# The RG-LRU mixer of a four-layer kernel: convolution through PSUM, Tanh for Sigmoid, low parts and the gelu product on GpSimd

## The reference

```python
def rglru_mixer(u, w_in, b_in, conv_w, conv_b, w_gx, b_gx, w_ga, b_ga, lam, w_out, b_out):
    proj = u @ w_in + b_in
    ybr = jax.nn.gelu(proj[..., :LRU_WIDTH])
    xbr = causal_dwconv(proj[..., LRU_WIDTH:], conv_w, conv_b)      # 4 taps
    xh = xbr.reshape(bsz, s, LRU_HEADS, LRU_BLOCK)                  # 10 heads of 128
    gx = sigmoid(einsum('bshi,hij->bshj', xh, w_gx).reshape(...) + b_gx)
    ga = sigmoid(einsum('bshi,hij->bshj', xh, w_ga).reshape(...) + b_ga)
    log_a = 8.0 * ga * log_sigmoid(lam)
    a_t = exp(log_a)
    b_t = sqrt(-expm1(2.0 * log_a)) * gx * xbr
    _, h = associative_scan(_linear_combine, (a_t, b_t), axis=1)    # h = a_t * h_prev + b_t
    return (h * ybr) @ w_out + b_out
```

## Time and profile before

| | us |
|---|---|
| median of three runs | 3145.37 |
| lowest and highest run | 3143.47, 3150.71 |
| the profiled execution, its own time | 3148.56 |
| its span | 3146.7 |
| TensorE busy | 2977.8 (95%) |
| VectorE busy | 1379.6 (44%) |
| ScalarE busy | 1194.0 (38%) |
| GpSimd busy | 1352.2 (43%) |

### The profile page before, as it was taken

One profiled execution on the slowest core, in us unless ns is written; L12 is line 12 of the kernel. 1 busy time (PEld: TensorE's weight loads), 2 busy tenths in 40 slices (PEclk: granted clock), 3 DMA queues, 4 the chain that ended last, 5 costly groups with the idle time before them and its releaser, 6 DMA issues.

```text
span 3146.7 us, 33766 instructions
## 1 busy us (share of the span) xinstructions
PE 2977.8 (95%) x13508; PEld 2440.9 (78%) x13508; DVE 1379.6 (44%) x2011; ACT 1194.0 (38%) x1658; POOL 1352.2 (43%) x724
## 2 busy tenths in 40 slices
PE   8899999999999788999999996999999989999998
PEld 6777777888887566888888785987888867778886
DVE  6655406523532683551352356653313345433132
ACT  5434436423433464542343432014323334343232
POOL 5333454444445366444444446005444432144443
PEclk9999999999999889999999997579999989999999
DMA  3211132232232222323332230002333321022322
GB/s 133 70 59 46 35 107 87 94 99 96 96 99 74 70 68 80 101 95 99 94 101 94 80 101 27 1 21 88 96 97 101 90 68 57 28 94 91 104 89 85
DMA packets 74172, 253.12 MB, mean 80 GB/s; under 512 B 8352, under 2 KB 8352, under 8 KB 74016
## 3 DMA queue, kind: packets, MB, share of 16 engines
q1 hardware_dynamic: 73008, 247.55, 24.4%
q10 hardware_dynamic: 1008, 3.41, 0.3%
HBM read 248.83 MB, written 2.10 MB: 80 GB/s over the span
## 4 chain that ended last, share of the span: by engine, by line
PE 86%; DVE 7%; ACT 3%; DMA 1%; issue 1%; POOL 1%; POOLq 0%; DVEq 0%; ACTq 0%; SPq 0%
PE bank L374 22%; PE bank L375 22%; PE bank L376 22%; PE bank L1660 3%; PE bank L396 2%; PE bank L397 2%; PE bank L398 2%; PE bank L855 1%; PE bank L857 1%; PE bank L856 1%; POOL wlo L2356 1%; PE bank L936 1%; DVE bank L1189 1%; DVE lth L1505 1%; ACT whi L319 1%
## 5 line engine op out<-in xcount | busy, mean ns | idle before, releaser
L2356 POOL TENSOR_TENSOR wlo<-raw,whi 128x1024 fp32r<-128x1024 f32 (+2 forms) x497 | 1133.5, 2283 | 1685.9 <-ACT whi L319 1685.8
L319 ACT ACTIVATE whi<-raw 128x1024 fp32r<-128x1024 f32 (+2 forms) x497 | 500.1, 1007 | 1126.5 <-DMA raw<-in_f_up 487.9
L374 PE MATMUL bank<-h_hi,whi 128*128 128x512 f32 x2240 | 880.2, 393 | 9.2 <-DVE h_lo L1956 3.4
L375 PE MATMUL bank<-h_lo,whi 128*128 128x512 f32 x2240 | 874.4, 390 | 0.0
L376 PE MATMUL bank<-h_hi,wlo 128*128 128x512 f32 x2240 | 873.4, 390 | 0.0
L374 PEld LDWEIGHTS bank<-h_hi,whi 128*128 128x128 f32 x2240 | 422.3, 189 | 102.1 <-DVE h_lo L1956 4.2
L375 PEld LDWEIGHTS bank<-h_lo,whi 128*128 128x128 f32 x2240 | 422.3, 189 | 89.2 <-issue 2.2
L376 PEld LDWEIGHTS bank<-h_hi,wlo 128*128 128x128 f32 x2240 | 422.3, 189 | 88.4
L374 PE MATMUL bank<-act_hi,whi 128*128 128x512 f32 x864 | 336.2, 389 | 0.9 <-POOL wlo L2356 0.9
L376 PE MATMUL bank<-act_hi,wlo 128*128 128x512 f32 x864 | 336.1, 389 | 0.0
L375 PE MATMUL bank<-act_lo,whi 128*128 128x512 f32 x864 | 336.1, 389 | 0.0
(11 more groups left out here) (451 smaller groups left out, 3802.9 us busy)
## 6 DMA issues: line engine op xcount, KB each, us to landing
raw<-in_f_up SPq DMA_DIRECT2D x216, 512.0 KB, 3.5
raw<-in_f_dn SPq DMA_DIRECT2D x64, 512.0 KB, 3.4
raw<-in_ssd_xbc SPq DMA_DIRECT2D x24, 512.0 KB, 3.5
raw<-in_f_dn SPq DMA_DIRECT2D x32, 384.0 KB, 3.0
raw<-in_lru_in SPq DMA_DIRECT2D x20, 512.0 KB, 3.5
raw<-in_ev_in SPq DMA_DIRECT2D x20, 512.0 KB, 3.5
raw<-in_f_dn SPq DMA_DIRECT2D x32, 320.0 KB, 2.9
raw<-in_ssd_z SPq DMA_DIRECT2D x16, 512.0 KB, 3.5
```

What stands on the lines that cost most here:

```text
L319: act.activation(whi[:, s, 0:WIDTH[u]], raw[:, s, 0:WIDTH[u]], ACT.Copy).then_inc(hi_done, 1)
L374: pe.matmul(out, wh, hi, start=kt == 0, stop=False)
L375: pe.matmul(out, wh, lo, start=False, stop=False)
L2356: pool.tensor_tensor(wlo[:, s, 0:n], raw[:, s, 0:n], whi[:, s, 0:n].bitcast(F32), ALU.subtract)\
```

## The change

- The convolution runs in the bank. ScalarE writes `ltap` with three zero columns ahead of it, waits for this, and writes the first tap with the bias back into the bank; VectorE adds three taps with the bank as one operand, and the last writes `xbr` and frees the bank.
- `low_x` moves from VectorE to GpSimd, and GpSimd's order in the stage's first part is written out around it.
- Sigmoid(x) becomes (1 + Tanh(x/2)) / 2, with the halves folded into the constants, `gated`, `decay` and `root`.
- `high_x` stands ahead of the weight split in ScalarE's order. Decays 0 to 3 move up among the x tiles, as do `one_minus` 0 and 1.
- The constants of lambda are computed in the SSD stage (VectorE: before tile 12 there) and kept in a place of their own. `lsq` moves to the place of another stage's tile.
- The product of scan and gelu moves to GpSimd, two blocks ahead of its low part. The scan is still written to SBUF.

The core of the diff (the lambda steps in the SSD stage, which are the old ones at new places, are cut):

```diff
-        ltap = at("ltap", BIG + 80 * KB, [P, 2, T])
-        lsq = at("lsq", BIG + 84 * KB, [P, 2, T])
+        ltap = at("ltap", BIG + 80 * KB, [P, 2, T + 4])
+        lsq = at("lsq", place["sqg"], [P, 2, T])
...
+        def lam_dve(dve, own):
...
+            own.link(dve.tensor_scalar(bias, bias, 0.5, None, ALU.mult))
+            own.link(dve.tensor_scalar(v0, v, 4.0, None, ALU.mult))
+            dve.tensor_scalar(u, v, -4.0, None, ALU.mult).then_inc(l_lam, 1)
...
+                elif t == 12:
+                    lam_dve(dve, own)
...
-            def sigmoids(g):
+            def tanhs(g):
...
-                        act.activation(b, b, ACT.Sigmoid, bias=col("lru_bgx", h)).then_inc(l_sg, 1)
+                        act.activation(b, b, ACT.Tanh, bias=col("lru_bgx", h), scale=0.5).then_inc(l_sg, 1)
                     else:
-                        act.activation(ga[:, h, :], b, ACT.Sigmoid, bias=col("lru_bga", h)).then_inc(st.free(t), 1)
+                        act.activation(ga[:, h, :], b, ACT.Tanh, bias=col("lru_bga", h), scale=0.5).then_inc(st.free(t), 1)
...
+            act.wait_ge(l_lam, 5)
             for j in range(NL):
                 st, t = l_in[j]
+                if j >= 2:
+                    high_x(j - 2)
                 if j in (5, 7, 9):
-                    sigmoids(j // 2 - 2)
+                    tanhs(j // 2 - 2)
                 act.wait_ge(l_u, j + 1)
                 w(act, l_x, j - 1)
-                act.activation(ltap[:, j % 2, :], st.bank(t)[:], ACT.Identity, bias=col("lru_bx", j)).then_inc(st.free(t), 1)
+                own.link(act.activation(ltap[:, j % 2, 3:T + 3], st.bank(t)[:], ACT.Identity, bias=col("lru_bx", j)))
+                act.activation(st.bank(t)[:], ltap[:, j % 2, 3:T + 3], ACT.Identity, bias=col("lru_conv", 5 * j + 4),
+                               scale=col("lru_conv", 5 * j + 3)).then_inc(l_tap, 1)
                 in_ahead(j)
-                if j >= 2:
-                    high_x(j - 2)
-            sigmoids(3)
+                if j in (6, 8):
+                    decay(j - 6)
+                    decay(j - 5)
             high_x(NL - 2)
+            tanhs(3)
             high_x(NL - 1)
-            act.wait_ge(l_lam, 4)
-            for k in range(3):
-                decay(k)
+            decay(4)
+            decay(5)
             in_ahead(10)
-            for k in range(3, 6):
-                decay(k)
-            in_ahead(11)
-            sigmoids(4)
             decay(6)
             decay(7)
-            in_ahead(12)
+            in_ahead(11)
+            tanhs(4)
             decay(8)
             decay(9)
+            in_ahead(12)
...
             def conv(j):
                 st, t = l_in[j]
-                st.freed(dve, t)
-                src, cv = ltap[:, j % 2, :], xbr[:, j, :]
-                own.link(dve.tensor_scalar(cv, src, col("lru_conv", 5 * j + 3), col("lru_conv", 5 * j + 4), ALU.mult,
-                                           ALU.add))
+                b = st.bank(t)[:]
+                dve.wait_ge(l_tap, j + 1)
                 for n in (1, 2, 3):
-                    ins = dve.scalar_tensor_tensor(out=xbr[:, j, n:T], in0=ltap[:, j % 2, 0:T - n],
-                                                   scalar=col("lru_conv", 5 * j + 3 - n), in1=xbr[:, j, n:T],
-                                                   op0=ALU.mult, op1=ALU.add)
+                    ins = dve.scalar_tensor_tensor(out=xbr[:, j, :] if n == 3 else b, in0=ltap[:, j % 2, 3 - n:T + 3 - n],
+                                                   scalar=col("lru_conv", 5 * j + 3 - n), in1=b, op0=ALU.mult, op1=ALU.add)
...
-                        ins.then_inc(l_x, 1)
...
+                        ins.then_inc(st.free(t), 1)
+                st.freed(dve, t)
+                dve.engine_nop().then_inc(l_x, 1)
...
-                own.link(dve.tensor_tensor_scan(out=lth[:, k, :], data0=ga[:, k, :], data1=xbr[:, k, :], initial=0.0,
-                                                op0=ALU.mult, op1=ALU.add))
-
-            def product(k):
-                dve.wait_ge(l_y, k + 1)
-                dve.tensor_tensor(lth[:, k, :], lth[:, k, :], ybr[:, k, :], ALU.mult).then_inc(l_h, 1)
+                dve.tensor_tensor_scan(out=lth[:, k, :], data0=ga[:, k, :], data1=xbr[:, k, :], initial=0.0,
+                                       op0=ALU.mult, op1=ALU.add).then_inc(l_sc, 1)
 
             for j in range(NL):
                 scale_x(j)
                 if j >= 1:
                     conv(j - 1)
-                if j >= 2:
-                    low_x(j - 2)
                 if j in (5, 7, 9):
                     gated(j // 2 - 2)
+                if j == 8:
+                    one_minus(0)
+                    one_minus(1)
             conv(NL - 1)
-            low_x(NL - 2)
-            low_x(NL - 1)
             gated(3)
-            for k in range(3):
-                one_minus(k)
+            one_minus(2)
+            one_minus(3)
             scale_y(0)
-            for k in range(3, 6):
-                one_minus(k)
+            one_minus(4)
+            one_minus(5)
             scale_y(1)
-            gated(4)
             one_minus(6)
             one_minus(7)
+            gated(4)
...
+            def low_x(j):
+                pool.wait_ge(l_hi, j + 1)
+                if j >= 3:
+                    l_gate[(j - 3) // 2].tile_ready(pool, 2 * ((j - 3) % 2) + 1)
+                pool.tensor_tensor(xb_lo[:, j % 3, :], xbr[:, j, :], xb_hi[:, j % 3, :].bitcast(F32), ALU.subtract)\
+                    .then_inc(l_lo, 1)
+
+            def lru_product(k):
+                pool.wait_ge(l_y, k + 1)
+                pool.wait_ge(l_sc, k + 1)
+                pool.tensor_tensor(lth[:, k, :], lth[:, k, :], ybr[:, k, :], ALU.mult).then_inc(l_h, 1)
+
             def lru_lows(first, end):
                 for k in range(first, end):
+                    if k + 2 < NL:
+                        lru_product(k + 2)
...
-            u = lows(u, l_in[10][0].u0 + RING)
-            lru_squares(0, 3)
+            u = lows(u, l_in[0][0].u0 + RING)
+            for j in range(NL):
+                if j >= 2:
+                    low_x(j - 2)
+                u = lows(u, u + (2 if j in (5, 7, 9) else 1))
+                if j in (6, 8):
+                    lru_squares(j - 6, j - 4)
+            low_x(NL - 2)
             u = lows(u, u + 1)
-            lru_squares(3, 6)
+            low_x(NL - 1)
+            lru_squares(4, 6)
+            u = lows(u, u + 1)
+            lru_squares(6, 8)
             u = lows(u, u + 2)
-            lru_squares(6, 8)
-            u = lows(u, u + 1)
             lru_squares(8, 10)
-            u = lows(u, u + 3)
+            u = lows(u, u + 4)
+            lru_product(0)
+            lru_product(1)
             lru_lows(0, 2)
             u = lows(u, u + 1)
             lru_lows(2, 4)
```

More of the change, by code:

```diff
@@ L806, in build_program @@
         Norm.count = dict(sq=NX, mm=SSD_G, rms=SSD_G, t=NX, hi=NX)
+        l_u, l_x, l_sg, l_tap, l_hi, l_lo = (sem("l_" + s) for s in ("scaled", "x", "sg", "tap", "hi", "lo"))
+        l_lam, l_sc, l_a, l_sq, l_q, l_s, l_y, l_h, l_ph, l_pl = (
+            sem("l_" + s) for s in ("lam", "scan", "a", "a2", "q", "s", "y", "h", "prod_hi", "prod_lo"))
         norm0 = pre("mix_pre", 0)
@@ L993, in ssd_pe @@
             post0.stat.pe(pe)
+        def lam_dve(dve, own):
+            lam = col("lru_lam", 0, NL)
+            v0, u, v, ln = (lam8[:, n, :] for n in range(4))
+            bias = col("lru_bgx", 0, 2 * NL)
+            dve.wait_ge(l_lam, 4)
+            own.link(dve.tensor_scalar(v, v, -1.0, 1e-30, ALU.add, ALU.max))
+            own.link(dve.reciprocal(v, v))
+            own.link(dve.tensor_tensor(ln, ln, u, ALU.mult))
+            own.link(dve.tensor_tensor(ln, ln, v, ALU.mult))
+            own.link(dve.tensor_scalar(v, u, -0.5, 1.0, ALU.mult, ALU.add))
+            own.link(dve.tensor_tensor(v, v, u, ALU.mult))
+            own.link(dve.tensor_tensor(ln, ln, v, ALU.max))
+            own.link(dve.scalar_tensor_tensor(out=v, in0=lam, scalar=0.0, in1=ln, op0=ALU.min, op1=ALU.subtract))
+            own.link(dve.tensor_scalar(bias, bias, 0.5, None, ALU.mult))
+            own.link(dve.tensor_scalar(v0, v, 4.0, None, ALU.mult))
+            dve.tensor_scalar(u, v, -4.0, None, ALU.mult).then_inc(l_lam, 1)
         def ssd_act(act, own):
@@ L1008, in dt_step @@
                     act.activation(acol[:, 0:1], col("a_log"), ACT.Exp).then_inc(dt_act, 1)
+                    act.activation(lam8[:, 0, :], col("lru_lam", 0, NL), ACT.Abs).then_inc(l_lam, 1)
+                    act.wait_ge(l_lam, 1)
+                    act.activation(lam8[:, 1, :], lam8[:, 0, :], ACT.Exp, scale=-1.0).then_inc(l_lam, 1)
                 elif t == 5:
@@ L1334, in lru_act @@
         def lru_act(act, own):
[L1336 to L1340, removed]
             def high_x(j):
@@ L1364, in decay @@
                 l_gate[k // 2].freed(act, 2 * (k % 2) + 1)
```

(23 more changed lines are left out.)

15 lines of the change are left out of this document (6 added, 9 removed).

## The result

| | before | changed |
|---|---|---|
| median of 20 runs each, us | 3147.71 | 3153.3 |
| lowest and highest | 3143.13, 3153.25 | 3145.94, 3157.28 |
| the profiled execution, its span | 3146.7 | 3148.1 |

The account below looks back on a forecast made before the run. VectorE was taken to bound both ends of the LRU stage. The output pair 24.3 us earlier, less 2.7 low clock and 0.3 lambda, gave 21.3: 3145.4 - 21.3 = 3124 us, range 3110 to 3136.

Parts of the forecast that it names:

- Unchanged spans cost nothing here: All code outside the edits was taken to keep its time, so the sum charged nothing for it.
- Case (e): Rival: later waits, for the pair's banks or `lru_out` weights at 1147.9, take back the gain; no change, chance 0.05.
- wait before gates(3): LRU stage: only tile 9 stands before gates(3), so TensorE waits 3.9 us, to 1082.4, against 8.2 before.
- convolution steps: LRU stage, VectorE: with one operand in the bank nothing is stretched, all steps 0.75 us, against up to 2.76.
- end of tile 19: LRU stage, TensorE: the last in-tile ends at 1144.5, 22.0 us earlier than before.
- last low part ends: LRU tail, GpSimd: the last low part ends at 1168.6 against 1192.96; the output pair is done 24.3 us earlier.
- low clock in the tail: TensorE's last block and the start of the next tile run at the low clock, +2.7 us (bounds 0 and 3.5).
- lambda steps in SSD: Lambda steps on VectorE before SSD tile 12, ahead of the `etot` wait, cost +0.3 us (bounds 0 and +2.5).
- the turns with the scans: LRU tail: GpSimd alternates with VectorE's scans 5 to 9, 1.8 us each, adding 9.0 to its queue.
- (b): Rival: no turns between GpSimd and scans in the tail, pair done 1161.3, no low clock; 33 us, 3112.4; chance 0.13.
- (c): Rival: ScalarE's queue is late, so gates(1) and gates(2) wait 3.9 + 1.9 each; 11.6 less, 3135.7; chance 0.18.
- (d): Rival: GpSimd bounds from the front, weight subtracts queue behind ten `low_x`, TensorE loses 35; 3159; chance 0.04.

Follow-up runs that it names:

- e2_lam_behind: The changed kernel with `lam8` laid behind `big`, so `big` stands at its old place: 3124.08 us, ratio 0.9933 to the kernel before.
- e5_lam_t16: e2_lam_behind with the lambda steps on VectorE ahead of SSD tile 16 instead of 12: 3121.81 us, ratio 0.9921 to the kernel before.
- e1_pad160: The kernel before with 160 unused bytes ahead of `big`, nothing else: 3175.86 us against 3145.26, ratio 1.0094.
- e3_pad96: The kernel before with 96 unused bytes ahead of `big`, nothing else: 3161.39 us, ratio 1.0052 to the kernel before.
- e4_all128: The kernel before with every large area moved from 64 above a multiple of 128 bytes to a multiple of 128: 3146.05 us, ratio 1.0002.
- e8_whi32: The kernel before with both weight areas, `raw` and `whi`, 32 bytes above a multiple of 64: 3214.06 us against 3146.94, ratio 1.0209.
- e11_whi_only: The kernel before with only the high weight halves, `whi`, 32 bytes above a multiple of 64: 3197.65 us against 3146.51, ratio 1.0163.

## Why the prediction was wrong

**The step that failed** is the first sentence of "The change, part by part": "Unchanged spans cost nothing here". It cost about 23 us: 19.5 in the feed-forward blocks, by the same 7.5 to 7.7 ns per matmul about 2.2 in the 288 of `ssd_out` (the SSD stage is 2.7 longer than in e2_lam_behind), and 1.4 in the 180 of `lru_out` (the six out-tiles behind the pair take 42.6 us against 41.3, a wait of 1.2 in each taken off). The spans of the two kernels, 3148.1 and 3122.8, differ by 25.3; the 3.8 of it in HGRN2 and S5 go with the granted clock there and are not counted (the kernel before, with `big` at the old place, has 376.6 in that stage). I read each edit for what runs, and not the line of places for what it shifts. None of the five cases contained it. Case (e), no change, came nearest in its number, but not in its reason: the waits that it named did not come.

**Point by point**, with 11.4 us taken off the changed kernel's times:

| step | forecast | measured |
|---|---|---|
| `scale_x(0)` | 1031.1 | 1031.1 |
| tile 4 starts | 0.6 earlier than 1036.4 | 1035.8 |
| wait before gates(3) | 3.9, to 1082.4 | 3.88, to 1082.4 |
| waits before gates(1), gates(2), gates(4) | none | none over 0.5 |
| convolution steps | 0.75 | 0.744 to 0.756 |
| end of tile 19 | 1144.5 | 1144.8 |
| last low part ends | 1168.6 | 1167.5 |
| low clock in the tail | 2.7 | none at its last blocks |
| lambda steps in SSD | +0.3 | about +2 (e5_lam_t16) |
| unchanged spans | 0 | +23 |

The walk through the hand-written orders held within 1.1 us at every mark of the table, because its durations were rows and its waits were read from the code. TensorE waited 7.24 us for unit 27's low half before the pair, which the walk had put at 1147.9 and which came at 1152.0. That mark was missed by 4 us, but it changed nothing, as GpSimd set the end. GpSimd's queue ran from 1140.14 to 1178.85, 38.7 us where 40.2 had been summed, so the turns with the scans cost 7.5 and not 9.0. The low clock in the tail was charged wrongly: it came where the pair starts, not where it ends. The granted clock was 0.50 from 1163.4 to 1166.0, where the first matmul after the 7.24 us wait took 0.79, as after the waits in the earlier trace rows, and 1.00 from 1170 on, where the last blocks follow waits of 0.6 and 1.1 us and issue at 0.24.

That e2_lam_behind met 3124 is partly luck. In its profile the LRU stage is 24.6 us shorter (21.6 forecast) and HGRN2 and S5 3.4 shorter (nothing forecast), while SSD is 1.5 longer (0.3 forecast) and the stretches between the stages 2.2 longer (nothing forecast). The span is 23.9 shorter, the median of the runs 21.2.

**Rivals.** (b) is refuted: the products took turns with the scans, 2.0 us each at first. By the lock that the Trainium skill states in "SBUF — State Buffer", section "Who interferes with whom", it could not occur, and this trace agrees (2.0 us beside scans, 1.29 for the last one after them). (c) and (d) did not come: no gate but gates(3) waited, and no in-tile from 12 to 19 waited for a weight half. The rule of "GPSIMD Engine Reference", section "Engine selection", in the Trainium skill, that elementwise work belongs on VectorE, held here in direction: with the product on VectorE the stage is 3.6 us shorter.

## What to carry to other kernels

When a new tile is put ahead of others in a hand-made layout, look at where every tile behind it comes to lie; here 160 bytes ahead of the matmuls' operands took back all that a well-working change had won, and laying them behind gave it back. When a profile shows a loss in code that was not touched, compare the durations of single instructions by operand first, by median and not by mean alone, and set the granted clock of the stage beside them; the lengths of untouched stages are the quickest check. A schedule walked on measured durations can be right to a microsecond and the total still wrong, so the untouched part needs a line of its own in the sum.

## What the runs showed of the hardware

- A 512-column matmul whose moving operand starts 32 bytes above a multiple of 64 in SBUF shows 397 ns instead of 389 in the changed kernel and e1_pad160 (392 to 399 in e3_pad96) and costs about 7.6 ns more (5.8 us over 768), at the full granted clock and with TensorE idle no longer than before. Multiples of 64 and of 128 are alike (e4_all128).
- The same holds for the stationary operand: 6.4 ns per matmul in e8_whi32 (14.8 us over the 2304 of feed-forward 0), 7.7 per matmul with `whi` in e11_whi_only, with the weight load's own record unchanged at 188 ns.
- The granted clock stayed at 1.00 across TensorE's waits of 0.6 and 1.1 us in the tail (1170 to 1179), and was 0.50 for the 2.6 us after its wait of 7.24 us.
- How much of a stage runs at the low clock differs between profiles though the code in it is the same: the 512 small matmuls of HGRN2 and S5 took 105.2 us at a grant of 0.65 and 112.6 at 0.61, with the same shortest and median durations.
